# Separate memory and a new order for a mixer's retention and attention, column groups and a new order for the cross attention

## The reference

```python
def token_mixer(h, ...):
    qa, ka, va, qb, kb, vb, gb, ca, cb = jnp.split(h @ w_in, splits, axis=-1)
    # A: 4 heads of 64, chunk-band softmax attention; samples read a cache of 256 past rows
    o_a = band_attention_prompt(qa, ka, va, rel_bias)      # or band_attention_sample
    # B: 4 heads, keys of 64, values of 128; carries a state s per sample
    o_b, new_s = retention(qb, kb, vb, ret_state, ret_gn_g)
    o_b = jax.nn.silu(gb) * o_b
    # C: convolution over 31 steps, layer norm, silu
    o_c, new_conv = conv_module(ca, cb, conv_state, ...)
    return jnp.concatenate([o_a, o_b, o_c], axis=-1) @ w_out, ...

# inside retention, for each block
att = jnp.einsum('nihd,njhd->nhij', qi, ki) * dmask
o = einsum('nhij,njhe->nihe', att, vi) + einsum('nihd,nhde->nihe', qi * q_dec, s)
s = s * s_dec + jnp.einsum('njhd,njhe->nhde', ki * k_dec, vi)   # then o is normalised by head

def cross_attention(h, mk, mv, wq, wo):                # 4 heads of 256
    q = (h @ wq).reshape(n, t, X_HEADS, X_HEAD_DIM)
    p = softmax(einsum('nqhd,nkhd->nhqk', q, mk) * X_HEAD_DIM ** -0.5)
    return einsum('nhqk,nkhd->nqhd', p, mv).reshape(n, t, -1) @ wo
```

## Time and profile before

| | |
|---|---|
| device time, median of 3 runs | 1863.4 us (1862.84 to 1864.01) |
| the profiled execution's own time | 1861.05 us |
| its span in the trace | 1859.2 us |
| TensorE busy | 1696.7 us (91%) |
| DVE, ACT, POOL busy | 958.8, 736.5, 124.3 us |
| TensorE's mean granted clock | 0.961 of full speed |

### The profile page before, as it was taken

How to read it: one execution, slowest core, us unless ns; L and a number is a source line. 1 busy time by engine, 2 the same in 40 slices (tenths; PEclk the granted TensorE clock), 3 DMA queues, 4 the chain that set the end, 5 groups by cost and what they waited for, 6 DMA issues and landing times.

```text
span 1859.2 us, 21936 instructions
## 1 busy us (share of the span) xinstructions
PE 1696.7 (91%) x7878; PEld 1254.9 (67%) x7878; DVE 958.8 (52%) x1427; ACT 736.5 (40%) x1044; POOL 124.3 (7%) x243
## 2 busy tenths in 40 slices
PE   6998799988898998999987998788999999999996
PEld 3454555756677788744546466577888888888885
DVE  1621333334322334218025233357888898888987
ACT  2114112422422323211131224334776777777775
POOL 2230110000000000030302000000000000000000
PEclk9999899999898999999988999987999999999998
DMA  7535334262532333242432432744998988988983
GB/s 258 167 92 174 114 105 158 80 249 95 178 101 80 136 113 124 90 119 89 150 127 94 158 136 91 272 154 163 313 316 290 325 297 298 321 306 293 320 303 140
DMA packets 176142, 343.47 MB, mean 185 GB/s; under 512 B 6939, under 2 KB 48173, under 8 KB 175809
## 3 DMA queue, kind: packets, MB, share of 16 engines
q1 hardware_dynamic: 163808, 319.31, 50.3%
q0 software_dynamic: 3920, 12.58, 2.2%
q10 hardware_dynamic: 8352, 10.75, 1.6%
HBM read 332.58 MB, written 11.90 MB: 185 GB/s over the span
## 4 chain that ended last, share of the span: by engine, by line
PE 83%; ACT 6%; DVE 5%; issue 3%; DMA 1%; POOL 0%; ACTq 0%; DVEq 0%; SPq 0%; POOLq 0%
PE bank L1082 21%; PE bank L1121 15%; PE bank L1122 14%; PE bank L1123 14%; PE bank L1069 4%; PE bank L1193 3%; PE bank L1099 2%; PE bank L1573 2%; ACT arena L1650 2%; DVE arena_parts L875 1%; ACT arena_parts L871 1%; DMA ring<-in_w_in 1%; PE bank L1199 1%; PE bank L1522 1%; PE bank L1551 1%
## 5 line engine op out<-in xcount | busy, mean ns | idle before, releaser
L1121 PE MATMUL bank<-arena_parts,features_parts 128*128 128x512 f32 (+1 forms) x960 | 373.3, 389 | 23.3 <-DVE arena_parts L746 9.5
L1122 PE MATMUL bank<-arena_parts,features_parts 128*128 128x512 f32 (+1 forms) x960 | 368.3, 384 | 0.0
L1123 PE MATMUL bank<-arena_parts 128*128 128x512 f32 (+1 forms) x832 | 325.3, 391 | 0.0
L875 DVE TENSOR_TENSOR arena_parts<-ring,arena_parts 128x1024 fp32r<-128x1024 f32 (+1 forms) x246 | 279.8, 1155 | 38.3 <-ACT arena_parts L871 33.4
L1082 PE MATMUL bank<-ring,features_T 128*128 128x512 f32 (+1 forms) x672 | 272.7, 568 | 2.8 <-ACT features_T L1650 2.8
L871 ACT ACTIVATE arena_parts<-ring 128x1024 fp32r<-128x1024 f32 (+1 forms) x246 | 243.5, 1007 | 67.4 <-PE bank L1123 64.1
L1082 PEld LDWEIGHTS bank<-ring,features_T 128*128 128x128 f32 x672 | 128.3, 192 | 143.2 <-issue 137.1
L1121 PEld LDWEIGHTS bank<-arena_parts,features_parts 128*128 128x128 f32 x960 | 183.3, 191 | 56.0 <-issue 16.5
L1650 ACT ACTIVATE arena<-bank 128x512 f32<-128x512 f32 (+3 forms) x160 | 85.0, 567 | 340.6 <-PE bank L1082 202.8
L1122 PEld LDWEIGHTS bank<-arena_parts,features_parts 128*128 128x128 f32 x960 | 183.3, 191 | 31.0
L1123 PEld LDWEIGHTS bank<-arena_parts 128*128 128x128 f32 x832 | 159.4, 192 | 32.2
(11 more groups left out here) (280 smaller groups left out, 1807.1 us busy)
## 6 DMA issues: line engine op xcount, KB each, us to landing
ring<-in_moe_w_up SPq DMA_DIRECT2D x41, 1024.0 KB, 6.7
ring<-in_moe_w_down SPq DMA_DIRECT2D x30, 1024.0 KB, 5.1
ring<-in_moe_w_gate SPq DMA_DIRECT2D x22, 1024.0 KB, 6.9
ring<-in_w_in SPq DMA_DIRECT2D x20, 1024.0 KB, 5.3
mem_kv<-in_moe_w_gate SPq DMA_DIRECT2D x20, 1024.0 KB, 5.3
ring<-in_cache_mem_k SPq DMA_DIRECT2D x16, 1024.0 KB, 6.8
ring<-in_cache_mem_v SPq DMA_DIRECT2D x16, 1024.0 KB, 7.0
ring<-in_moe_w_gate SPq DMA_DIRECT2D x20, 768.0 KB, 6.1
```

The lines of the kernel that those rows point to most:

```text
L875: nc.vector.tensor_tensor(self.part(p, 1), self.raw(p), self.part(p, 0).bitcast(F32), ALU.subtract).then_inc(self.split, 1)
L1121: nc.tensor.matmul(out, left[0], right[0], start=start, stop=False)
L1122: nc.tensor.matmul(out, left[0], right[1], start=False, stop=False)
L1123: return nc.tensor.matmul(out, left[1], right[0], start=False, stop=stop)
```

## The change

In the mixer, `attT` and `attS` get memory that is free at that time (in `features_T`), and `q0` and `ks` become smaller and lie over the convolution's inputs, which are read by then. `q0` holds 32 columns for each pair of samples in place of 128, and the four pairs' products write four column groups of the bank; `ks` holds two samples' masks in place of eight, and the four pairs' products take four row groups and four banks. The order of TensorE's program changes: `aB`, `aS` and `nsP` stand between the rounds of sample scores, `yc` and the prompt's `oB` follow, `oS` and `sS` change the column group at each matmul, `ocT` comes ahead of `obT`, and the second half of `out` runs tile by tile with one norm tile turned inside it. ACT takes all exponentials after the last key copy. In the cross attention, `xss` and `xv` change the column group at each matmul, turned keys have four places rather than two, all key slabs come ahead of all value slabs, the four slabs of `o` get places of their own and are loaded by `load_o`, and the tiles of `o` are mixed with the last samples' work. SP starts the next slabs of the feed-forward parts earlier.

```diff
-        m.at = at0
-        attT = cut(m.take(BH * TOK), h=BH)
-        attS = cut(m.take(BH * P), h=BH)
-        q0 = cut(m.take(BH * 512), h=BH)
-        ks = m.take(BH * 512).rearrange("p (h n d) -> p h n d", h=BH, n=NS)
+        attT = cut(fT_[:, 2 * TOK:6 * TOK], h=BH)
+        attS = cut(fT_[:, 6 * TOK:6 * TOK + BH * P], h=BH)
...
+        q0 = up_[:, 0:BH * P].rearrange("p (h j c) -> p h j c", h=BH, j=4)
+        ks = us_[:, 0:BH * P].rearrange("p (h i d) -> p h i d", h=BH, i=2)
...
-                                ins = nc.tensor.matmul(out, q0[:, h, j * P:(j + 1) * P], s0[:, j, h, :],
-                                                       start=False, stop=(j == 3))
+                        ins = nc.tensor.matmul(b[32 * j:32 * j + 32, h * P:(h + 1) * P], q0[:, h, j, :], s0[:, j, h, :],
+                                               start=False, stop=True)
...
-                        for t in range(3):
-                            right = (past[:, 2 * (n % 4) + t, k * P:(k + 1) * P] if t < 2
+                    for t in range(3):
+                        for n2 in range(2):
+                            for k in range(2):
+                                n, row = 2 * r + n2, 64 * n2 + 32 * k
...
-                for h in range(BH):
-                    b = begin("nsS", l, h)
-                    for j in range(4):
-                        ins = nc.tensor.matmul(b[:, j * P:(j + 1) * P], ks[:, h, 2 * j:2 * j + 2, :],
-                                               proj[:, 2, VB + h * P:VB + (h + 1) * P], start=True, stop=True)
+                b = [begin("nsS", l, j) for j in range(4)]
+                for h in range(BH):
+                    for j in range(4):
+                        ins = nc.tensor.matmul(b[j][:, h * P:(h + 1) * P], ks[32 * j:32 * j + 32, h, :, :],
...
-                wait_emptied(dve, "oS", l)
-                st.did(V.memset(q0, 0.0))
...
-                wait_emptied(pool, "oS", l)
+                pool.wait_ge(s_conv, 2 * (l + 1))
...
-                    if n == 3:
-                        exp_prompt()
-                    if n % 2 and n >= 5:
-                        exp_sample((n - 5) // 2)
+                wait_filled(act, "nsP", l)
+                st.emptied(A(spr[0:64, :], bank[BANK[("nsP", l)][0]][0:64, :], ACT.Copy), "nsP", l)
+                act.wait_ge(s_max, 6 * l + 2)
...
+                    for i in range(4):
+                        for n2 in range(2):
+                            for hp in range(2):
+                                g = 32 * (2 * n2 + hp)
+                                n = 2 * r + n2
+                                ins = nc.tensor.matmul(b[g:g + 32, 0:256], qxb[:, 4 * hp + i, n, :],
+                                                       kTs[:, n % 4, 4 * hp + i, :], start=(i == 0), stop=(i == 3))
...
-        product("wx_o", ("o", l), l, full, NT)
+        for n in range(NS):
+            out.append(("cache_mem_k", "mem", (l, n), ("kTs", l, n, 3)))
+        for n in range(NS):
+            out.append(("cache_mem_v", "mem", (l, n), ("xv", l, n // 2)))
...
+            def load_o(l, m):
+                if m == 4:
+                    wait_filled(sp, "q", l, 1, NT - 1)
+                elif m == 5:
+                    wait_filled(sp, "xo", l, XH - 1)
+                    sp.wait_ge(s_mvo, 16 * (l + 1))
+                else:
+                    wait_filled(sp, "xss", l, m - 4)
...
+                for after, m in ((("cache_mem_k", 5), 4), (("cache_mem_v", 1), 5), (("cache_mem_v", 5), 6),
+                                 (("cache_mem_v", 7), 7)):
+                    if how == "mem" and (name, where[1]) == after:
+                        load_o(where[0], m)
...
+        one(("xpTs", l, 3), "a")
+        one(("o", l, 0, 0), "v")
+        one(("xvT", l, 2), "v")
+        one(("xv", l, 3), "v")
+        one(("o", l, 0, 1), "v")
         one(("xvT", l, 3), "v")
-        product(("o", l), 2, NT, "v")
-        norm(3 * l + 2)
+        one(("o", l, 1, 0), "v")
+        one(("o", l, 0, 2), "v")
+        one(("o", l, 1, 1), "v")
+        norm(3 * l + 2, (0,))
+        one(("o", l, 1, 2), "v")
+        norm(3 * l + 2, (1, 2))
```

More of the change, by code:

```diff
@@ L257, in product @@
             for half in range(2):
-                last = tiles - 1 if half or (c == 0 and key[0] == "in") else 0
+                last = tiles - 1 if half or (key[0], c) in (("in", 0), ("out", 1)) else 0
                 reader = ("split", l, 2 * c + half + (4 if key[0] == "o" else 0)) if key[0] in ("q", "o") else key + (c, last)
@@ L966, in w_high @@
[L966 removed]
+            if m < 4:
+                s = WHERE[("split", l, m)]
+                act.wait_ge(slab_in[s % R], 16 * (s // R + 1))
+            else:
+                act.wait_ge(s_oslab[m - 4], 16 * (l + 1))
+            if m == 3:
+                wait_filled(act, "q", l, 0, NT - 1)
+            elif m == 4:
+                wait_filled(act, "xs", l, 3)
+            nc.scalar.activation(part(l, m, 0), whole(l, m), ACT.Copy).then_inc(s_whigh, 1)
@@ L1060, in slab @@
             def slab(name):
-                s = at[1]
-                at[1] += 1
+                s = next(s for s in range(len(SLABS)) if s not in taken and SLABS[s][3][0] != "split")
+                taken.add(s)
                 assert SLABS[s][0] == name, (SLABS[s], name)
@@ L1271, in _, with last_out @@
             for l in range(DEPTH):
+                def last_out():
+                    wt = [slab("w_out").rearrange("p (k n) -> p k n", k=4) for _ in range(2)]
+                    for t in range(NT):
+                        if t == NT - 1:
+                            norm(3 * l + 1, (0,))
+                        b = begin("out", l, 1, t)
+                        for k in range(KC):
+                            ins = nc.tensor.matmul(b[:, :], oT_at(k, t), wt[k // 4][:, k % 4, :],
+                                                   start=(k == 0), stop=(k == KC - 1))
+                        end(ins, "out", l, 1, t)
                 norm(3 * l, (0,))
@@ new lines, in _ @@
+                group_stats(0)
+                group_stats(1)
+                group_scale(0)
+                group_scale(1)
+                group_stats(2)
+                group_scale(2)
+                for j in range(4):
+                    wait_filled(dve, "nsS", l, j)
+                    for h in range(BH):
+                        st.did(V.scalar_tensor_tensor(
+                            s0[:, j, h, :], s0[:, j, h, :], GAMMA[h] ** TS,
+                            bank[BANK[("nsS", l, j)][0]][:, h * P:(h + 1) * P], ALU.mult, ALU.add),
+                            emptied["v"] if h == BH - 1 else None)
+                    assert st.last[1] == DRAIN[("nsS", l, j)][1]
```

885 lines of the change are left out of this document (483 added, 402 removed).

## The result

The changed kernel takes 1752.7 us, the median of four runs from 1748.96 to 1759.46; the kernel before took 1863.7 beside it. The ratio is 0.9408 (95% interval 0.9374 to 0.9442). The profiled execution took 1748.96, against 1861.05 before: 112.1 us less. The profiled execution is the fastest of the four; where their spread of 10 us comes from is not settled, and stages are therefore compared by windows of the profiled executions.

The account below looks back on a forecast made before the run. TensorE, with 83% of the chain, bounds the kernel through waits, lower clock and work that could run side by side. Savings of 32.0 + 1.5 + 23.3 + 1.1 = 57.9 us a layer, 115.8 for two, give 1748; range 1728 to 1784.

Parts of the forecast that it names:

- signs of being wrong: Profile checks: mixer wait over 2 us, `xss` at 4.5, several `xv` waiting over 3, `oB` bank waits, clock below 0.9.
- A, the mixer: Memory keys' product to out-projection: 97.1 us falls to 65.1 (61.1 work, 4.0 waits), 32.0 saved a layer.
- `oB` term: Sample's `oB` in the mixer, four column groups: between 1.8 and 4.4 us a layer, taken at 1.8.
- B, out to q: Out-projection to q product, 45.88 us: residual add and norm hidden under matmuls, 1.5 saved a layer, bounds 0 and 1.85.
- C, the cross attention: From q's end to o's end: 115.2 us falls to 91.9, 23.3 saved a layer.
- the landing: Cross attention: the fourth values' slab lands 7.1 us after issue (4.8 alone, 10.4 worst), giving a 2.7 us wait.
- the second rival: Cross attention: values' slabs land at 10.4 us rather than 7.1, costing 20 us, total 1768; chance 0.17.
- D, the tail: After o's end only the last tile's norm remains: 0 to 2 us saved a layer, taken at 1.1.
- the groups give nothing: Mixer and cross attention: grouped jobs take as long as before, 17.5 us a layer, total 1783; chance 0.10.
- DVE late in the mixer: Mixer: POOL's work delays DVE and TensorE waits for banks, 5 to 8 us a layer, 1758 to 1764; chance 0.12.
- The clock: Mixer and cross attention: TensorE gets 1.2 GHz through the rearranged stretches, total 1973; chance 0.03.
- it doesn't do what it says: Whole change: waits move but stay as long, time within a few us of 1863; chance 0.02.

Follow-up runs that it names:

- experiment 5: The changed kernel with ACT issuing the output transfer of the prompt's memory keys four copies later: 1750.2 us, ratio 0.9389 to the kernel before.
- experiment 9: The changed kernel with the split weight slabs moved to a multiple of 128 bytes: 1738.1 us, ratio 0.935 to the kernel before.
- experiment 10: The changed kernel with 96 unused bytes a partition giving the table of constants its old length: 1751.0 us, ratio 0.9401 to the kernel before.
- experiment 3: The changed kernel with `xss` and `oS` back in runs of one column group: 1765.4 us, ratio 0.9482 to the kernel before.
- experiment 7: The changed kernel with ACT's exponentials put back between the key copies: 1758.7 us, ratio 0.9434 to the kernel before.

## Why the prediction was right, and where it was off
The forecast was 1748 and the median is 1752.7; the sum of terms was 115.8, the stages gave 116.4, and 112.1 arrived. That the stages come so close to the sum is partly luck: B gave 4.2 more than its term, A and C gave 1.8 and 2.6 less. Two of the signs of being wrong came true in part: a wait over 2 us stands in layer 0's mixer (2.94), and one `xv` a layer waits over 3 us (3.08 and 3.90). Term by term, for two layers:

- *A, the mixer: 64.0 forecast, 62.2 measured.* TensorE's work was 62.5 a layer, not 61.1. `oS` took 2.62 (3.0 forecast), `nsS` 1.10 (1.3), the sample's `oB` 2.90 (1.8). The `oB` term left out the way back: after the first head, whose unit of 128 columns took 0.22, each unit behind a group of 32 columns took 0.42, so 0.20 more for each of them; and the four groups together took 0.35, not 0.22. The Trainium skill (TensorEngine Tiling (Array Packing), "Key Properties") says that a change between tiling modes drains the array first; the 0.42 against 0.22 agrees with it. Of the waits, the bank that DVE still reads cost 0.36 (1.4 forecast) and the hand-over to the out-projection 1.01 (0.8), and the clock was 1.00. The `aB` wait of 2.94 and 1.39 was not in the sum, so that the waits came to 4.3 and 2.8 where 4.0 was forecast, but of other kinds. The prediction followed DVE and ACT, but not the output transfer that DVE's mask waits for: before, it was issued 3.06 us behind the second slab of the memory values' weights and landed in 4.3; after, 0.27 behind it, and it landed in 9.56 (experiment 5).
- *B, out to q: 3.0 forecast, 7.2 measured.* The bounds were too low: they held only TensorE's idle time inside the window (45.88 less 44.03), whereas its granted clock of 0.96 went up to 1.00 as well. Busy time fell from 44.03 to 41.75 and 41.97.
- *C, the cross attention: 46.6 forecast, 44.0 measured, and q another 0.7 longer.* The grouped scores are as forecast (1.86 to 1.93 for 1.9), and the wait ahead of o is 0.36. The failed size is the values': 9.9 us in all, where 2.7 a layer and half a us after it were taken. The step that failed is the landing. The walk through the order was right: the fourth values' slab was issued 38.2 us behind q's end in both layers (39.2 forecast). But it landed in 9.2 and 9.5 us, not 7.1, where all slabs of the stretch share some 400 GB/s (median 8.5 and 9.0), so the second `xv` waited 3.08 and 3.90. And the sum had no wait for the first pair, whose second slab came 1.56 and 1.03 too late. The pairs behind these were covered as forecast (0.38 in layer 0, nothing in layer 1). This is the second rival's mechanism at about a fifth of its price (some 3.5 us over forecast, not 20).
- *D, the tail: 2.2 forecast, 3.0 measured.*
- *Not in the sum:* 5.0 us lost in the experts and 0.7 in q to the place of the arena (experiments 9 and 10), 0.1 at the start, and 1.6 gained in layer 0's dense part and the next in-projection. That the constants' length could matter outside the mixer was nowhere considered.

The rivals: *the groups give nothing* fell by experiment 3, whose `xss` of 4.59 against 1.93 differs by nothing but the order of its matmuls. The Trainium skill's rule on it (TensorE: Matmul & The Clock Gate, Part 3, "The mechanism") does not hold here: in `xss` the weights of four column groups are loaded within 20 ns while the first group's matmul runs, and column groups on the same rows do overlap, if a group's matmuls don't follow one another four at a time. *DVE late in the mixer* did not come as described: no wait at the banks of `oB` beyond 0.36, and POOL did not hold TensorE up. *The clock* was 0.98 to 1.00 in the rearranged stretches, and *it doesn't do what it says* fell with the three waits. That the cover of the exponentials was worth 3.98 stays unproven: experiment 7 shows some 1.8 at full clock.

## What to carry to other kernels
Matmuls that use column groups gain by the order in which they are issued: alternate the groups, at most two of one group in a row. A wait that is taken away starts transfers sooner and closer together, so work out the bytes over the new, shorter stretch and look for output transfers that a later writer waits for. After a change of a table's or buffer's length, compare the pace of an untouched product before and after.

## What was not expected of the hardware
The pace of split products of 512 columns depends on where their operands lie: one per 0.2276 us with the split slabs at a multiple of 128 bytes, 0.2310 and 0.2331 with the slabs 32 bytes behind a multiple of 64, by where the arena starts, at a granted clock of 1.00 in each. Some 14 us hung on it: against the changed kernel, experiment 9 is 1.6 us shorter in the two q products, 4.3 from layer 0's dense part to the next mixer, and 8.3 in the experts. Which operand's place counts, or their distance, isn't separated: with the arena back and the slabs 32 bytes off, experiment 10 has 0.2312. The plain f32 products of 512 columns, which don't read the split slabs, kept their pace (0.429 us a record in each). And one output of 1 MB landed in 4.1 to 4.3, 5.9 to 6.2 or 7.9 to 9.6 us, when it was issued 3.06, 1.4 or 0.27 us behind a slab's load.
